# One of the four first-key one-hots of a group gathered by GpSimd from an identity matrix in DRAM

## The chip, the cores and the metric

The kernel runs on one core of a Trainium2 chip, in one launch. The metric is the device time of that launch in microseconds. All data are float32.

## The reference, cut to what matters

One encoder block over x of 1024 tokens by 1024: a Mamba-2 head group and an HGRN2 head group share an input and an output projection, then comes a PEER layer that picks experts by product keys, then a last RMSNorm. The change lies in the PEER layer:

```python
def peer_ffn(x, w_query, sub_keys, u_table, v_table):
    q = (xt @ w_query).reshape(t, PEER_HEADS, 2, PEER_HALF)
    s = jnp.einsum('thpd,hpnd->thpn', q, sub_keys)
    s_top, i_top = lax.top_k(s, PEER_TOPK)
    ...
    expert = idx1 * PEER_KEYS + idx2
    gate = jax.nn.softmax(c_top, axis=-1)
    def block(args):
        xb, eb, gb = args
        u = u_table[eb]
        hid = gelu(jnp.einsum('td,thkd->thk', xb, u)) * gb
        return jnp.einsum('thk,thkd->td', hid, v_table[eb])
```

There are 8 heads, 128 keys on each side (16384 experts) and 16 experts per token and head, so each token picks 128 experts, each with a first key, a second key and a gate.

## The kernel before, in words

The program runs stage after stage, each in its own block of instruction streams: input_norm, ssd, hgrn, mix_out, peer. The order of work within a stage is written out by hand, and engines wait on semaphores. The span of 3635 us divides into about 1127 us up to the end of hgrn, mix_out to about 1559 us, and peer.

**mix_out** multiplies by w_out (loaded by SP, L1313, after two small loads, L1309 and L1310), adds x, and routes the first 512 tokens on VectorE. GpSimd scatters the gates of token block 0 into the DRAM tensor sel (L1574), 16 indirect DMAs of 128 elements per head, and waits for each head's before the next.

**peer** treats the two halves of the tokens in different ways. The first 512 (blocks 0 to 3) go densely: for each first key e of 128, TensorE multiplies the tile u_cols[e] with the tokens (L1919), ScalarE takes gelu, VectorE multiplies by a tile of gates read from sel (L2125), and TensorE multiplies by v_cols (L1932) and VectorE adds (L2132). The other 512 go sparsely: GpSimd gathers, for a pick of each of 128 tokens, the 4 KB rows of u_rows (u_row, L1828) and v_rows (v_row, L1835) into two rings of 5 buffers; VectorE makes a dot product (L2138) and adds gate times row (L2149). Both run side by side, slot by slot, 256 slots.

Before the slots stands the **hot stage**, which the change touches. It fills sel for token blocks 1 to 3 (MB = 3), as a dense matrix of gates over first and second key for each token. A group j of 96 (M_GROUPS) takes 4 tokens. The partition is a pick of the token, the free index a key.

- VectorE (hot, from L2104) makes hot_a: one compare of 512 columns, 4 tokens by 128 keys, 1 where the key is the pick's first key (L2109). Then it makes three of the four hot_b: 1 where the key is the second key, times the gate (L2113).
- ScalarE (hot_last, L1972 and L1975) makes the fourth hot_b out of Abs and Relu.
- TensorE (L1900) multiplies the transposed hot_a with hot_b for each of the four tokens: a 128x128 matrix of gates in ps_o.
- ScalarE (place_out, L1988 and L1991) copies each half of it into a staging buffer. In its stream stand, for each group: place_out(j, 0), hot_last(j + 2), place_out(j, 1).
- SP stores a staging buffer of 2 MB to sel after each 16 groups (L1805), twice. hot_a, hot_b and ps_o have two buffers: VectorE's group j waits until TensorE has done group j - 2, and TensorE's group j until ScalarE has copied out group j - 2.

A block of 32 groups is one block of 128 tokens. Its picks are turned by TensorE (turn_picks, L1887) and copied by ScalarE (pick_copy, L1964 and L1965) into pickedT; the first two at the start, the third at group 40. After groups 24 and 60 VectorE routes a unit of the sparse half (about 10 us each), and TensorE and ScalarE stand still.

GpSimd does nothing in the hot stage but five u_row (from 1608 us, once the routing after group 24 has given their indices). Then it waits for the last store of sel, sel_out[3], and issues v rows. SP loads the first three tiles of u_cols into ut[0], ut[1], ut[2] during the last block (L1799); ut[2] is the tensor ut2. After the last stores it loads va (L1810). ScalarE loads the first tiles of sel (L2018) once all stores have landed.

Of the kernel before, what the change touches and what calls it, by code (L numbers as in the profile page):

```python
# [8 lines left out]
F32 = mybir.dt.float32  # L9
# [49 lines left out]
RING = 5  # L59
OB = 3  # L60
# [328 lines left out]
def ssd(nc, w, w_in, w_ssd, par, w_hg, lb_logits, C, hnT, Y, spent, hw, H):  # L389
# [4 lines left out]
    with ExitStack() as ctx:  # L394
# [3 lines left out]
        primed = []  # L398

        def plain_sem(name):  # L400
            return ctx.enter_context(nc.semaphore("ssd_" + name))
# [265 lines left out]
        def _(dve):  # L667
# [130 lines left out]
            groups(dve, body)  # L798


def hgrn(nc, w_hg, C, hnT, Y, osq, ysq, sel, sel_zeroed, H):
# [6 lines left out]
    with ExitStack() as ctx:  # L808
# [299 lines left out]
class Route:  # L1108
# [3 lines left out]
    def __init__(self, nc, ctx):  # L1112
# [32 lines left out]
        self.scattered, self.negated = sem("scattered"), sem("negated")  # L1145
# [93 lines left out]
def mix_out(nc, x, w_out, mix_w, ffn_w, w_route, sel, sel_zeroed, C, Y, osq, ysq, xnT, R):  # L1239
# [4 lines left out]
    with ExitStack() as ctx:  # L1244
# [61 lines left out]
        def _(sp):  # L1306
# [344 lines left out]
def peer(nc, w_route, u_cols, v_cols, u_rows, v_rows, fin_w, sel, C, Y, osq, hnT, R, out):  # L1651
# [4 lines left out]
    with ExitStack() as ctx:  # L1656
# [35 lines left out]
        hot_a = [mflat[:, i * 512:(i + 1) * 512].rearrange("p (q c) -> p q c", q=4) for i in range(2)]  # L1692
        hot_b = [mflat[:, 1024 + i * 512:1024 + (i + 1) * 512].rearrange("p (q c) -> p q c", q=4) for i in range(2)]
# [4 lines left out]

        stage = [wide(va[:]), wide(vb), Y[:, 0:4, D:MIX], vr[:, 0:4, :]]
# [23 lines left out]
        sel_out = [sem(f"sel_out{i}") for i in range(4)]  # L1723
        x_turned, x_out = sem("x_turned"), sem("x_out")
# [99 lines left out]
        def _(pool):  # L1824
# [14 lines left out]
            for r in range(RING):  # L1839
                u_row(r)  # L1840
# [12 lines left out]
        def _(pe):  # L1853
# [38 lines left out]
            for j in range(M_GROUPS):  # L1892
# [203 lines left out]
        def _(dve):  # L2096
# [7 lines left out]
            def hot(j):  # L2104
# [4 lines left out]
                nc.vector.tensor_tensor(hot_a[j % 2], R.count[:].unsqueeze(1).to_broadcast([P, 4, KEYS]),  # L2109
                                        pickedT[:, b % 2, 0, t:t + 4].unsqueeze(2).to_broadcast([P, 4, KEYS]),  # L2110
# [101 lines left out]
def block_program(nc, x, ln_w, w_ssd, par, w_hg, lb_logits, w_out, mix_w, ffn_w, w_route, u_cols, v_cols, u_rows, v_rows,  # L2212
                  fin_w, sel, out):
    with ExitStack() as ctx:
# [6 lines left out]
        with nc.sbuf_tensor("reset", [P, SEQ], F32) as reset, nc.sbuf_tensor("lmask", [P, LEVELS + 1, P], F32) as lmask:  # L2221
            C["reset"], C["lmask"] = reset, lmask
            with nc.sbuf_tensor("w_group", [P, KT, SSD_COLS], F32) as w_group, ExitStack() as held:
# [4 lines left out]
                ssd(nc, w_group, group_in, w_ssd, par, w_hg, lb_logits, C, hnT, Y, spent, hw, H)  # L2228
                hgrn(nc, w_hg, C, hnT, Y, osq, ysq, sel, sel_zeroed, H)
        R = Route(nc, ctx)  # L2230
        mix_out(nc, x, w_out, mix_w, ffn_w, w_route, sel, sel_zeroed, C, Y, osq, ysq, hnT, R)
        peer(nc, w_route, u_cols, v_cols, u_rows, v_rows, fin_w, sel, C, Y, osq, hnT, R, out)
# [59 lines left out]
```

## Time and profile before

| | |
|---|---|
| runs | 3635.82 us median of 3 (3635.19 to 3636.2) |
| profiled execution | 3637.07 us, its span 3635.3 us |
| TensorE (PE) busy | 3447.0 us, 95% |
| VectorE (DVE) | 2821.6 us, 78% |
| ScalarE (ACT) | 1075.0 us, 30% |
| GpSimd (POOL) | 1428.6 us, 39% |
| DMA | 829.65 MB, 228 GB/s on average |

PE is TensorE's matmuls, PEld its weight loads, SPq SyncE's DMA issues. L12 is line 12 of the kernel. Times in the rows are microseconds from the start of the span. The figure in brackets behind a row of the timeline is how long the engine had been idle before it, and what ended that. "issue" is time in which an engine waited for nothing that the profile shows. A duration on the timeline runs until the result is written, so the next instruction can start before it ends.

### The profile page before, as it was taken

The numbers are of one execution on the slowest core, as the hardware profiler recorded it, in microseconds if no ns is written. First come the engines' busy times: TensorE is split into PE (matmuls) and PEld (weight loads), VectorE is DVE, ScalarE is ACT, GpSimd is POOL, SyncE is SP. The second block draws the span as 40 slices with busy tenths as digits, with TensorE's granted clock in tenths as the row PEclk, the third lists the DMA queues.
The fourth block names the chain that finished last, engine by engine and source line by source line (L and its number), as shares of the span: only waits on it lengthen the run. The fifth ranks groups of instructions, "written<-read, shape, count | busy, mean of one in ns | idle before, by whom it ended". The sixth has DMA issues, their size and how long they took to land.

```text
span 3635.3 us, 39991 instructions
## 1 busy us (share of the span) xinstructions
PE 3447.0 (95%) x11593; PEld 1977.6 (54%) x11593; DVE 2821.6 (78%) x6530; ACT 1075.0 (30%) x2717; POOL 1428.6 (39%) x1233
## 2 busy tenths in 40 slices
PE   7999989999996999677899999999999999999998
PEld 4666667777774566456444444444444444444443
DVE  2466676777773489889698888987888889888897
ACT  3233344435452222278121112111211122121212
POOL 1000000000001277400466566655666666665664
PEclk9999999999997999889999999999999999999999
DMA  3111012001003233245999999999999999999998
GB/s 111 30 36 35 0 61 79 23 23 35 25 10 136 50 75 75 34 132 173 388 387 377 392 386 386 377 391 351 389 375 388 389 390 378 376 394 378 387 377 329
DMA packets 313936, 829.65 MB, mean 228 GB/s; under 512 B 41504, under 2 KB 145056, under 8 KB 305056
## 3 DMA queue, kind: packets, MB, share of 16 engines
q0 software_dynamic: 165888, 537.01, 39.9%
q1 hardware_dynamic: 125104, 227.45, 17.2%
q10 hardware_dynamic: 22768, 63.18, 4.5%
q8 instruction: 69, 1.13, 0.1%
q14 instruction: 107, 0.88, 0.1%
HBM read 789.73 MB, written 37.81 MB: 228 GB/s over the span
## 4 chain that ended last, share of the span: by engine, by line
PE 44%; issue 6%; DVE 4%; DMA 2%; POOL 1%; another core or an unknown queue 0%; ACT 0%; DVEq 0%; ACTq 0%; POOLq 0%
PE peer_ps_o L1932 21%; PE peer_ps_d L1919 20%; PE peer_ps_q L1860 2%; DMA peer_vr<-in_v_rows,peer_index 2%; DVE Y L2149 1%; DVE peer_ur L2138 1%; DVE peer_mt L2109 0%; POOL peer_ur L1828 0%; DVE peer_mt L2113 0%; POOL peer_vr L1835 0%; DMA peer_ur<-in_u_rows,peer_index 0%; PE peer_ps_s L1870 0%; DVE Y L2166 0%; DVE route_hit L1209 0%
## 5 line engine op out<-in xcount | busy, mean ns | idle before, releaser
L1828 POOL DMA_INDIRECT peer_ur<-in_u_rows,peer_index x512 | 569.4, 1112 | 606.3 <-DVE peer_ur L2138 396.8
L2149 DVE SCALAR_TENSOR_TENSOR Y<-peer_vr,peer_hid,Y 128x1024 f32<-128x1024 f32 x512 | 657.1, 1283 | 103.1 <-DMA peer_vr<-in_v_rows,peer_index 97.9
L1835 POOL DMA_INDIRECT peer_vr<-in_v_rows,peer_index x512 | 588.8, 1150 | 331.8 <-issue 149.0
L2138 DVE SCALAR_TENSOR_TENSOR peer_ur<-peer_ur,Y 128x1024 f32<-128x1024 f32 x512 | 628.0, 1227 | 9.7 <-DMA peer_ur<-in_u_rows,peer_index 7.9
L1919 PE MATMUL peer_ps_d<-hnT,route_ut 128*128 128x512 f32 x1376 | 598.5, 592 | 0.0
L1932 PE MATMUL peer_ps_o<-peer_va,Y 128*128 128x512 f32 x1024 | 445.0, 594 | 12.8 <-DVE Y L2125 12.8
L1932 PE MATMUL peer_ps_o<-hnT,Y 128*128 128x512 f32 x1024 | 442.6, 592 | 0.0
L1919 PEld LDWEIGHTS peer_ps_d<-hnT,route_ut 128*128 128x128 f32 x1376 | 261.3, 190 | 327.7 <-issue 327.7
L1932 PEld LDWEIGHTS peer_ps_o<-peer_va,Y 128*128 128x128 f32 x1024 | 194.9, 191 | 253.8 <-issue 236.1
L1932 PEld LDWEIGHTS peer_ps_o<-hnT,Y 128*128 128x128 f32 x1024 | 193.5, 190 | 238.2 <-issue 238.2
L1919 PE MATMUL peer_ps_d<-hnT,peer_ut 128*128 128x512 f32 x672 | 295.3, 592 | 0.0
L2006 ACT ACTIVATE peer_act_out<-peer_dots 128x2 f32<-128x2 f32 x256 | 51.2, 200 | 796.2 <-DVE peer_ur L2138 775.4
L1999 ACT ACTIVATE Y<-peer_ps_d 128x512 f32<-128x512 f32 x128 | 76.4, 597 | 672.2 <-PE peer_ps_d L1919 652.2
L1574 POOL DMA_INDIRECT sel<-route_ut,mo_sel_index x128 | 210.1, 1641 | 159.0 <-DVE route_ut L1217 89.1
L1375 PE MATMUL mo_ps_h<-mo_w,mo_yT 128*128 128x512 f32 x512 | 225.9, 599 | 8.2 <-DMA mo_w<-in_w_out 7.1
L512 PE MATMUL ssd_ps_piece<-hnT,w_group 128*128 128x512 f32 x512 | 226.8, 596 | 6.9 <-ACT hw L595 5.1
L1559 POOL IOTA mo_count_u<- 128x128 uint32 x1 | 0.2, 240 | 592.2 <-POOLq L808 592.2
L1919 PEld LDWEIGHTS peer_ps_d<-hnT,peer_ut 128*128 128x128 f32 x672 | 127.4, 190 | 159.3 <-issue 159.3
L494 POOL TENSOR_TENSOR ssd_awide<-ssd_a,tri 128x512 f32<-128x512 f32 x32 | 34.5, 1079 | 450.2 <-PE ssd_ps_rows L556 403.1
L894 PE MATMUL hg_ps_piece<-hnT,hw 128*128 128x512 f32 x448 | 199.7, 599 | 4.3 <-ACTq L1017 4.3
L898 PE MATMUL hg_ps_piece<-hw,hnT 128*128 128x256 f32 x896 | 198.0, 379 | 0.0
L898 PEld LDWEIGHTS hg_ps_piece<-hw,hnT 128*128 128x128 f32 x896 | 168.1, 190 | 21.7
(329 smaller groups left out, 4894.6 us busy)
## 6 DMA issues: line engine op xcount, KB each, us to landing
route_ut<-in_u_cols SPq DMA_DIRECT2D x86, 512.0 KB
peer_va<-in_v_cols SPq DMA_DIRECT2D x16, 2048.0 KB
peer_mt<-sel ACTq DMA_DIRECT2D x64, 512.0 KB
hnT<-in_v_cols SPq DMA_DIRECT2D x16, 2048.0 KB
peer_ut<-in_u_cols SPq DMA_DIRECT2D x42, 512.0 KB
route_wk<-in_w_route ACTq DMA_DIRECT2D x14, 1024.0 KB
hnT<-in_w_route SPq DMA_DIRECT2D x9, 1024.0 KB
route_wk<-in_w_route SPq DMA_DIRECT2D x9, 1024.0 KB
```

Of the source, the lines that this page charges most:

```text
L512: mm = nc.tensor.matmul(bank, w[:, k, i * P:(i + 1) * P], hnT[:, half, k, :], start=(k == 0), stop=(k == KT - 1))
L894: mm = nc.tensor.matmul(bank, w[:, kt, p * P:(p + 1) * P], hnT[:, half, kt, :], start=(kt == 0), stop=(kt == KT - 1))
L898: mm = nc.tensor.matmul(bank[:, 0:2 * P], hnT[:, half, kt, cols(p - 2)], w[:, kt, 2 * P:4 * P], start=(kt == 0), stop=(kt == KT - 1))
L1375: mm = nc.tensor.matmul(ps_h[:, half, :], yT[:, k, :], w[:, k, half * 512:(half + 1) * 512], start=(k == 0), stop=(k == MT - 1))
L1574: pool.indirect_dma_start(sel.rearrange("a i q two (t o) -> (a i q two t) o", o=1), bass.IndirectOffsetOnAxis(ap=sel_index[:, h, k:k + 1], ...
L1828: pool.indirect_dma_start(ur[:, r % RING, :], None, u_rows, bass.IndirectOffsetOnAxis(ap=index[:, r // TOPK % 4, r % TOPK:r % TOPK + 1], a ...
L1835: pool.indirect_dma_start(vr[:, r % RING, :], None, v_rows, bass.IndirectOffsetOnAxis(ap=index[:, r // TOPK % 4, r % TOPK:r % TOPK + 1], a ...
L1919: mm = nc.tensor.matmul(ps_d[:, e % 2, :], ut[e % UT][:, k, :], xT[:, k, :], start=(k == 0), stop=(k == KT - 1))
L1932: mm = nc.tensor.matmul(ps_o[:, o % OB, :], ht(e, tb), v_tile(e, half), start=(j == 0), stop=(j == GE - 1))
L1999: nc.scalar.activation(ht(e), ps_d[:, e % 2, :], ACT.Gelu).then_inc(gelu_done, 1)
L2138: nc.vector.scalar_tensor_tensor(out=ur[:, s, :], in0=ur[:, s, :], scalar=1.0, in1=Y[:, b, D:MIX], op0=ALU.mult, op1=ALU.mult, accum_out=d ...
L2149: nc.vector.scalar_tensor_tensor(out=hb, in0=vr[:, s, :], scalar=hid[:, c:c + 1], in1=hb, op0=ALU.mult, op1=ALU.add).then_inc(comb_done, 1)
```

## The change

The 128x128 identity, which lies in SBUF, is stored to a DRAM tensor eye at the beginning of mix_out, ahead of the loads of w_out. In the hot stage VectorE compares 384 columns for three tokens of a group; the fourth first-key one-hot is a gather by GpSimd: partition p gets row first_key[p] of eye, 512 bytes. The gathered one-hots go into a ring of 8 buffers, which lie in ut2. So the third tile of u_cols is loaded only after the last group's product. At the first group of each block VectorE copies the first keys as integers into first_place, and GpSimd waits for that copy. The five u_row move behind hot rows 86, 88, 90, 92 and 94 of GpSimd's stream. TensorE waits for the gathered row, too. The new semaphores need room: hgrn's SP clears those of ssd.

```diff
@@ peer, sync
                     sp.wait_ge(pick_turned, MB)
-                    for e in range(UT):
+                    for e in range(UT - 1):
                         sp.dma_start(ut[e], u_cols[e]).then_inc(u_in[e], 16)
...
             for i in range(2):
                 sp.wait_ge(sel_out[i], sel_stores(i))
+            sp.wait_ge(sel_made, M_GROUPS)
+            sp.dma_start(ut[UT - 1], u_cols[UT - 1]).then_inc(u_in[UT - 1], 16)
             sp.dma_start(va[:], v_cols[0, 0]).then_inc(v_in[0], 16)
@@ peer, gpsimd
-            for r in range(RING):
-                u_row(r)
+            def hot_row(j):
+                b, t = j // (P // 4), j % (P // 4) * 4 + 3
+                if t == 3:
+                    pool.wait_ge(place_ready, b + 1)
+                need(pool, sel_made, j - HOTS + 1)
+                pool.indirect_dma_start(hots[:, j % HOTS, :], None, eye,
+                                        bass.IndirectOffsetOnAxis(ap=first_place[:, b % 2, t:t + 1], axis=0)
+                                        ).then_inc(got_hot[j % HOTS], 16)
+
+            pool.wait_ge(R.eye_out, 16)
+            for j in range(M_GROUPS):
+                hot_row(j)
+                if j >= M_GROUPS - 2 * RING and j % 2 == 0:
+                    u_row((j - M_GROUPS) // 2 + RING)
             pool.wait_ge(sel_out[3], sel_stores(3))
@@ peer, tensor
                 need(pe, staged, 2 * (j - 1))
+                pe.wait_ge(got_hot[j % HOTS], 16 * (j // HOTS + 1))
                 for q in range(4):
-                    mm = nc.tensor.matmul(ps_o[:, j % 2, q * P:(q + 1) * P], hot_a[j % 2][:, q, :], hot_b[j % 2][:, q, :],
+                    first = hot_a[j % 2][:, q, :] if q < 3 else hots[:, j % HOTS, :]
+                    mm = nc.tensor.matmul(ps_o[:, j % 2, q * P:(q + 1) * P], first, hot_b[j % 2][:, q, :],
                                           start=True, stop=True)
@@ peer, vector
-                nc.vector.tensor_tensor(hot_a[j % 2], R.count[:].unsqueeze(1).to_broadcast([P, 4, KEYS]),
-                                        pickedT[:, b % 2, 0, t:t + 4].unsqueeze(2).to_broadcast([P, 4, KEYS]),
+                if t == 0:
+                    nc.vector.tensor_copy(first_place[:, b % 2, :], pickedT[:, b % 2, 0, :]).then_inc(place_ready, 1)
+                nc.vector.tensor_tensor(hot_a[j % 2][:, 0:3], R.count[:].unsqueeze(1).to_broadcast([P, 3, KEYS]),
+                                        pickedT[:, b % 2, 0, t:t + 3].unsqueeze(2).to_broadcast([P, 3, KEYS]),
                                         ALU.is_equal).then_inc(hot_a_ready, 1)
@@ mix_out, sync
             sp.dma_start(fw, ffn_w).then_inc(s_in, 16)
+            sp.dma_start(eye, C["ident"][:]).then_inc(R.eye_out, 16)
@@ hgrn, sync
             prime(sp, primed)
+            for s in used:
+                sp.sem_clear(s)
```

HOTS is 8, RING is 5, UT is 3.

## Rows read from the trace of the kernel before

**Rows 1.** The page's busy part, and TensorE's waits from 1721 to 1900 us (total, times, longest).

```profile
PE 3447.0 (95%) x11593; PEld 1977.6 (54%) x11593; DVE 2821.6 (78%) x6530; ACT 1075.0 (30%) x2717; POOL 1428.6 (39%) x1233
...
PE peer_ps_o L1932 <- DVE Y L2125: 9.7, 2, 7.9
```

**Rows 2.** Windows: from:to, length, each engine's busy us (instructions), granted clock, DMA share, GB/s.

```profile
1620.00:1661.00 41.00, 32.88 (x236) 28.18 (x235) 40.57 (x118) 40.00 (x119) 0.00 (x0) 1.00 0.71 205
```

**Rows 3.** Timeline of one group: start us, duration us, engine, line, operation, output<-input, count.

```profile
1640.99 0.38 ACT L1991 ACTIVATE peer_va<-peer_ps_o 128x256 f32<-128x256 f32 x1
1641.07 0.68 DVE L2109 TENSOR_TENSOR peer_mt<-route_count,peer_pickedT 128x512 f32<-128x512 f32 x1
...
1641.25 1.13 PE L1900 MATMUL peer_ps_o<-peer_mt 128*128 128x128 f32 x8 [0.30 <-DVE peer_mt L2113]
1641.27 0.39 ACT L1972 ACTIVATE peer_mt<-route_count,peer_pickedT 128x128 f32<-128x128 f32 x1
1641.67 0.85 DVE L2113 TENSOR_SCALAR peer_mt<-route_count,peer_pickedT 128x128 f32<-128x128 f32 x3
1641.70 0.49 ACT L1975 ACTIVATE peer_mt<-peer_mt,peer_pickedT 128x128 f32<-128x128 f32 x1
1642.10 0.36 ACT L1991 ACTIVATE hnT<-peer_ps_o 128x256 f32<-128x256 f32 x1
1642.42 0.38 ACT L1991 ACTIVATE peer_va<-peer_ps_o 128x256 f32<-128x256 f32 x1
```

**Rows 4.** Groups by form, 1530 to 1730 us: count, busy us, mean ns, idle before, releasers.

```profile
L2109 DVE TENSOR_TENSOR peer_mt<-route_count,peer_pickedT 128x512 f32<-128x512 f32 x96 | 66.1, 689 | 6.1 <-PE peer_ps_o L1900 4.5 <-ACT peer_pickedT L1965 1.3
```

**Rows 5.** Timeline of VectorE, ScalarE and TensorE at the stage's beginning.

```profile
1559.91 0.36 DVE L2172 CAST route_ut<-peer_first_key 128x384 f32<-128x384 uint32 x1
...
1560.31 0.56 DVE L2173 SCALAR_TENSOR_TENSOR route_ut<-route_ut 128x384 f32<-128x384 f32 x1
...
1561.89 0.27 ACT L1965 ACTIVATE peer_pickedT<-peer_ps_t 128x128 f32<-128x128 f32 x1
...
1564.71 5.26 PE L1900 MATMUL peer_ps_o<-peer_mt 128*128 128x128 f32 x24 [1.65 <-ACT peer_mt L1975]
```

**Rows 6.** Timeline: VectorE ends a dot product, GpSimd, already waiting, starts a gather.

```profile
1749.72 0.08 DVE L2138 DVE_READ_ACCUMULATOR peer_ur<-peer_ur,Y 128x1 f32 x1
...
1750.57 1.24 POOL L1828 DMA_INDIRECT peer_ur<-in_u_rows,peer_index  x1 [2.81 <-DVE peer_ur L2138]
```

**Rows 7.** GpSimd's timeline while it scatters: two issues that waited for earlier ones to land.

```profile
1271.06 1.89 POOL L1574 DMA_INDIRECT sel<-route_ut,mo_sel_index  x1 [2.27 <-DMA sel<-route_ut,mo_sel_index]
...
1339.94 1.54 POOL L1574 DMA_INDIRECT sel<-route_ut,mo_sel_index  x1 [4.98 <-DMA sel<-route_ut,mo_sel_index]
```

**Rows 8.** GpSimd's timeline, 1608 to 1615 us; VectorE's products there (min/median/max ns); page's software queue.

```profile
1608.39 1.54 POOL L1828 DMA_INDIRECT peer_ur<-in_u_rows,peer_index  x1 [89.74 <-DVE peer_index L2101]
...
1612.80 0.94 POOL L1828 DMA_INDIRECT peer_ur<-in_u_rows,peer_index  x1 [0.30 <-issue]
...
1614.04 1.37 POOL L1828 DMA_INDIRECT peer_ur<-in_u_rows,peer_index  x1 [0.30 <-issue]
...
L2113 DVE TENSOR_SCALAR peer_mt<-route_count,peer_pickedT x12: 339/342/476, 1609.0 to 1615.0; 128x128 f32<-128x128 f32 x12
...
q0 software_dynamic: 165888, 537.01, 39.9%
```

**Rows 9.** GpSimd's timeline: the first v row.

```profile
1739.35 0.94 POOL L1835 DMA_INDIRECT peer_vr<-in_v_rows,peer_index  x1 [123.94 <-DMA sel<-peer_vr]
```

**Rows 10.** Windows at the end of the stage.

```profile
1705.00:1720.00 15.00, 12.10 (x88) 10.29 (x86) 15.00 (x45) 14.64 (x44) 0.00 (x0) 1.00 0.98 291
...
1720.00:1722.00 2.00, 1.20 (x9) 1.04 (x9) 2.00 (x3) 1.16 (x4) 0.00 (x0) 1.00 0.04 16
```

**Rows 11.** SP's timeline at mix_out's beginning, and TensorE's waits from 1100 to 1240 us.

```profile
1127.97 0.43 SPq L1310 DMA_DIRECT2D route_ut<-in_ffn_w  x1
...
PE mo_ps_h L1375 <- DMA mo_w<-in_w_out: 7.1, 1, 7.1
```

More of the change, by code:

```diff
@@ L59 @@
 RING = 5
+HOTS = 8
 OB = 3
@@ L396, in sb @@
             return ctx.enter_context(nc.sbuf_tensor("ssd_" + name, shape, dt))
-        primed = []
+        primed, used = [], []
         def plain_sem(name):
-            return ctx.enter_context(nc.semaphore("ssd_" + name))
+            used.append(ctx.enter_context(nc.semaphore("ssd_" + name)))
+            return used[-1]
         def sem(name):
@@ L798, in _, with hgrn @@
             groups(dve, body)
-def hgrn(nc, w_hg, C, hnT, Y, osq, ysq, sel, sel_zeroed, H):
+    return used
+def hgrn(nc, w_hg, C, hnT, Y, osq, ysq, sel, sel_zeroed, H, used):
     with ExitStack() as ctx:
@@ L1144, in __init__ @@
             sem("best_ready"), sem("gates_ready"), sem("routed"), sem("gated"))
-        self.scattered, self.negated = sem("scattered"), sem("negated")
+        self.scattered, self.negated, self.eye_out = sem("scattered"), sem("negated"), sem("eye_out")
 D_CHOSEN, D_GATE, D_FIRST, D_SECOND = range(4)
@@ L1236, in now, with mix_out @@
         self.hold()
-def mix_out(nc, x, w_out, mix_w, ffn_w, w_route, sel, sel_zeroed, C, Y, osq, ysq, xnT, R):
+def mix_out(nc, x, w_out, mix_w, ffn_w, w_route, eye, sel, sel_zeroed, C, Y, osq, ysq, xnT, R):
     with ExitStack() as ctx:
@@ L1648, in _, with peer @@
             gate_of(DU - 1)
-def peer(nc, w_route, u_cols, v_cols, u_rows, v_rows, fin_w, sel, C, Y, osq, hnT, R, out):
+def peer(nc, w_route, u_cols, v_cols, u_rows, v_rows, fin_w, eye, sel, C, Y, osq, hnT, R, out):
     with ExitStack() as ctx:
@@ L1692, in peer @@
         hot_a = [mflat[:, i * 512:(i + 1) * 512].rearrange("p (q c) -> p q c", q=4) for i in range(2)]
+        hots = ut2[:].rearrange("p k c -> p (k c)").rearrange("p (s c) -> p s c", c=P)
         hot_b = [mflat[:, 1024 + i * 512:1024 + (i + 1) * 512].rearrange("p (q c) -> p q c", q=4) for i in range(2)]
@@ L1697, in wide @@
             return t.rearrange("p k c -> p (k c)").rearrange("p (e d) -> p e d", d=D)
+        first_place = first_key[:, 0:2 * P].rearrange("p (b t) -> p b t", b=2)
         stage = [wide(va[:]), wide(vb), Y[:, 0:4, D:MIX], vr[:, 0:4, :]]
@@ L1723, in peer @@
         sel_out = [sem(f"sel_out{i}") for i in range(4)]
+        got_hot, place_ready = [sem(f"got_hot{i}") for i in range(HOTS)], sem("place_ready")
         x_turned, x_out = sem("x_turned"), sem("x_out")
@@ L2212, in block_program @@
 def block_program(nc, x, ln_w, w_ssd, par, w_hg, lb_logits, w_out, mix_w, ffn_w, w_route, u_cols, v_cols, u_rows, v_rows,
-                  fin_w, sel, out):
+                  fin_w, eye, sel, out):
     with ExitStack() as ctx:
@@ L2227, in block_program @@
                 spent = input_norm(nc, x, ln_w, w_ssd, C, hnT, w_group, group_in)
-                ssd(nc, w_group, group_in, w_ssd, par, w_hg, lb_logits, C, hnT, Y, spent, hw, H)
-                hgrn(nc, w_hg, C, hnT, Y, osq, ysq, sel, sel_zeroed, H)
+                used = ssd(nc, w_group, group_in, w_ssd, par, w_hg, lb_logits, C, hnT, Y, spent, hw, H)
+                hgrn(nc, w_hg, C, hnT, Y, osq, ysq, sel, sel_zeroed, H, used)
         R = Route(nc, ctx)
-        mix_out(nc, x, w_out, mix_w, ffn_w, w_route, sel, sel_zeroed, C, Y, osq, ysq, hnT, R)
-        peer(nc, w_route, u_cols, v_cols, u_rows, v_rows, fin_w, sel, C, Y, osq, hnT, R, out)
+        mix_out(nc, x, w_out, mix_w, ffn_w, w_route, eye, sel, sel_zeroed, C, Y, osq, ysq, hnT, R)
+        peer(nc, w_route, u_cols, v_cols, u_rows, v_rows, fin_w, eye, sel, C, Y, osq, hnT, R, out)
 def laid_out(inputs):
@@ L2287 @@
     out = nc.dram_tensor("out_0", [1, SEQ, D], F32, kind="ExternalOutput").ap()
+    eye = nc.dram_tensor("eye", [P, P], F32).ap()
     sel = nc.dram_tensor("sel", [KEYS, KEYS // 2, DB * P // SELB, 2, SELB], F32).ap()
-    block_program(nc, sel=sel, out=out, **args)
+    block_program(nc, eye=eye, sel=sel, out=out, **args)
     r = run_bass_kernel_spmd(nc, [{"in_" + n: a for n, a in arrays.items()}], core_ids=[0])
```

## The prediction

> **What bounds the kernel now.** I read the page's first two parts, then the times of the stage that the change touches, then one group of that stage instruction by instruction, then the waits behind it. Over the whole span TensorE is busy 95% and VectorE 78% [rows 1], but that average says little about the stretch after 1562 us, in which the 96 groups of one-hots are made. In 41 us of it VectorE is busy 40.57 us and ScalarE 40.00, GpSimd not at all, TensorE 32.88 [rows 2]. So VectorE looks like the bound, and ScalarE stands 0.6 us in 41 behind it: both lie at their limit.
>
> One group shows why [rows 3]. VectorE starts the 512-wide compare at 1641.07 and the first of the three products at 1641.67; the whole stretch of [rows 2] holds 118 VectorE instructions, four to a group, so a group comes every 41 / 29.5 = 1.39 us; I use 1.40. ScalarE's four operations start at 1641.27, 1641.70, 1642.10 and 1642.42, and the round closes 0.28 us later, as from 1640.99 to 1641.27: 0.43 + 0.40 + 0.32 + 0.28 = 1.43, of which some is waiting. Its busy share says how much: 1.0 us free in 41, or 0.03 per group, so ScalarE's own round is about 1.37 us. TensorE's round with ScalarE is no shorter: a product starts at 1641.25, the first copy-out at 1642.42 (1.17 later), the second 1.11 after that, done 0.36 later, then the product two groups on: 2.64 us and a hand-over of about 0.1 for two groups, again 1.37 each.
>
> **The change, part by part.**
>
> *VectorE's compare.* 384 columns in place of 512. The 512-wide form takes 0.689 us [rows 4], and its time goes with its width (a 384-wide two-input operation took 0.56 [rows 5]): 0.13 us less per group, 12.8 us over 96 groups if VectorE alone set the pace (96 is the count in [rows 4]). It doesn't: from 1.40 the group can fall to ScalarE's 1.37 and no further. That is 0.03 x 96, **-3.0 us**. Bounds: -3.5 with the four groups after the two routing pauses, where VectorE works alone, and 0 if ScalarE keeps 1.40.
>
> *The three copies into first_place*, one per block of 32 groups. A 128x384 cast took 0.36 us [rows 5], so about 0.2 for 128 columns. They fall in VectorE's new slack; what they cost is the head of the gather's chain, counted next. Queued behind a copy is the compare of its own group.
>
> *The first gather of each block.* GpSimd now issues 96 gathers of 128 rows of 512 bytes. Within a block it runs up to 8 groups ahead, but at groups 0, 32 and 64 it must wait for place_ready, which VectorE gives only after group j-2 has left TensorE. The chain from VectorE's start: copy 0.2; hand-over from VectorE's end to a waiting GpSimd 0.77 (1749.80 to 1750.57), the issue 1.24 [rows 6]; landing. No row shows a 64 KB gather landing. The nearest is the scatter of as many rows: GpSimd, waiting for its landing, sat idle 2.27 us, 0.77 of it hand-over, so 1.5 [rows 7]. Taken as 1.5; bounds 0.5 (a load that costs little beyond its bytes) and 4.2 (the longest such wait of the scatter, 4.98, less the hand-over). With 0.1 for TensorE: 3.8 us. TensorE would have taken that group 1.55 us after VectorE's start (0.60 + 0.85 + 0.1 [rows 3]). Each of groups 32 and 64 is late by 2.25 us: **+4.5**, bounds +2.4 and +10. Group 0: picked at 1562.16, product at 1564.71 [rows 5], gathered row at 1562.2 + 3.8 = 1566.0: **+1.3**, bounds +0.3 and +4. Behind a late product stand ScalarE's copy-out and VectorE's group after next, both double-buffered, so nothing is won back.
>
> *GpSimd's pace.* Five gathers of 4 KB rows were issued in this very stage, from 1608.39 to 1614.04 [rows 8]: 1.41 us apart on average, the last step 1.24. They go by the row, not by its length: 165888 packets for 1152 indirect transfers, 144 each, of 4 KB and of 4 bytes alike. I take 1.27, near the last step, since the first holds a wake-up; it is below TensorE's 1.37, and a lead grows by 0.10 us per group.
>
> *The five gathers of u rows.* Before, they ran in the pause at 1608 to 1615 [rows 8], where nobody waited. Now one goes after each of hot rows 86, 88, 90, 92 and 94. From hot row 86 to 95 GpSimd issues 14 times, 17.8 us, where TensorE wants nine groups, 12.3 us: 5.5 short. The lead since group 64 is 22 x 0.10 = 2.2. **+3.3**, bounds +2.2 (1.24 a piece) and +7.4 (1.41, no lead).
>
> *The u tile and the end of the stage.* The third u_cols load now waits for the last product and goes on SP behind the last stores and ahead of va, which comes later by it; TensorE takes that tile third. Its 512 KB at the software queue's 537 MB / (0.399 x 3635 us) = 370 GB/s [rows 8] is 1.4 us, moved behind the stores. The u rows (2.6 MB, 7.1 us at 370) and the last dozen hot rows (0.8 MB, 2.7 us at 291) come into a stretch in which the DMA engines are busy 0.98, with a gap of 2 us from 1720 [rows 10]. 7.1 + 2.7 - 1.4 - 2 - 3.3 (the stage is longer by that) leaves 3.1 us by which the last stores may land later, and GpSimd's first v row, which started at 1739.35, waits for just those, as do the first sel tiles [rows 9]. TensorE stalls later for 9.7 us on VectorE's multiply, two times [rows 1]; there is no spare time there, so what DMA is late may pass on. I take **+2.0** of 3.1, because part of the gathers' packets fit between stores; bounds 0 and +6.
>
> *Storing the identity* takes one SP issue ahead of w_out, 0.43 us, and TensorE waited 7.1 us for that load [rows 11]: **+0.4**, bounds 0 and +0.6. The sem_clears stand on SP while heads run; SP's next load there waits for TensorE anyway: 0, and some 3 us on SP if that cover were gone.
>
> **Sum**: -3.0 + 4.5 + 1.3 + 3.3 + 2.0 + 0.4 = **+8.5 us**. The profiled execution took 3637.07 us for a span of 3635.3 and lies 1.25 above the median 3635.82; set on the median this is 3644.3.
>
> *A rule against this change.* In the hot stage, with GpSimd gathering, VectorE's products showed 339 / 342 / 476 ns (min, median, max) where they otherwise stay near 340, and GpSimd's issues 0.94 to 1.54 us [rows 8]: they touch each other, now and then. The Trainium skill (SBUF — State Buffer, "Who interferes with whom") says that a tensor_scalar in a two-port mode holds a port pair that GpSimd needs to write descriptors, and that the second to come is blocked to the end of the instruction. By that rule the three products of each group would shut GpSimd out for part of 0.77 us in every 1.37. The trace agrees only in part: the last spacing is still the bare 1.24.
>
> **The rivals.**
>
> *GpSimd sets the pace (0.16).* If each gather costs the mean of the five in this stage, 1.37 + 0.30 after the last included, (1615.71 - 1608.39) / 5 = 1.46 us, it decides from 1.40 upward: 84 groups without a stored lead lose 0.06 each, 5.0; the u rows cost 14 x 1.46 - 9 x 1.40 = 7.8; nothing is gained at VectorE. 5.0 + 7.8 + 4.5 + 1.3 + 2.0 + 0.4 = +21.0, 3656.8. For it: the sample is from this stage. Against: its first step holds a wake-up. This is the mechanism of the skill's rule above.
>
> *Everything lands in the shadow (0.20).* All lower bounds: -3.5 + 2.4 + 0.3 + 2.2 = +1.4, 3637.2. For it: the load is small. Against: the scatter's 2.27.
>
> *VectorE was the whole bound (0.12), not slower than before.* If ScalarE's round shortens once VectorE is out of the way (it decides below about 1.30 us per group), the full 12.8 us are earned; the smallest latencies, 2.7, go off, and the u rows cost 17.4 - 9 x 1.27 - 0.7 = 5.3: -4.8, 3631.0; with the u rows hidden too it is -10.1. For it: VectorE's 40.57 of 41. Against: ScalarE's starts leave 0.03 us free per group. That the narrower compare isn't shorter is excluded by [rows 5].
>
> **How the numbers follow.** The forecast's own case has 0.52 and spreads over +4 to +15. A measurement of this kernel tells 0.2%, 7.3 us, from no change. Slower by more: 0.40 of the forecast's case and 0.16 of the GpSimd case, 0.56. Within: 0.12 of the forecast's, 0.20, and 0.05 of the last, 0.37. Faster by more: the rest of the last, 0.07. The range 3634 to 3657 takes in the shadow case, the forecast's whole spread and half of the GpSimd case; what is left out is most of the last rival and the other half, about 0.2.
>
> **What would show it.** In the changed profile: the compare near 0.55 us; ScalarE, not VectorE, without idle time in the stage, groups 1.37 us apart; three waits of TensorE's hot product for a DMA into the hots, some 1 to 2 us, at groups 0, 32 and 64, and more of them in the last ten groups; GpSimd's steps near 1.27; sel's last store landing 8 us later or more; the stall on VectorE's product around 1808 no shorter. I am wrong if those waits are absent, if the group falls well below 1.37, or if GpSimd's steps exceed 1.40.

## The result, and the profile after

The changed kernel took **3668.34 us** (median of 6, 3663.95 to 3671.78) against 3636.01 (median of 6, 3634.16 to 3640.13) in the same set: +32.3 us, a ratio of 1.0081 [1.007, 1.0091]. The forecast was 3644.3, +8.5, with a range from 3634 to 3657: slower, as said, but nearly four times as much. The profiled execution took 3668.46 us for a span of 3666.6; before it was 3637.07 and 3635.3.

The page's busy part, then the groups by form from 1560 to 1760 us (count, busy us, mean ns, idle time before and its releasers), of the changed kernel:

```profile
PE 3461.5 (94%) x11593; PEld 1989.4 (54%) x11593; DVE 2819.2 (77%) x6533; ACT 1076.4 (29%) x2717; POOL 1528.2 (42%) x1329
...
L1855 POOL DMA_INDIRECT peer_ut<-eye,peer_first_key x96 | 101.4, 1056 | 113.8 <-DVE peer_first_key L2135 85.0 <-issue 17.4 <-PE peer_ps_o L1925 11.4
...
L2140 DVE TENSOR_SCALAR peer_mt<-route_count,peer_pickedT 128x128 f32<-128x128 f32 x288 | 87.7, 362 | 0.0
L2136 DVE TENSOR_TENSOR peer_mt<-route_count,peer_pickedT 128x384 f32<-128x384 f32 x96 | 53.6, 558 | 30.0 <-PE peer_ps_o L1925 28.0
```

The compare fell from 689 to 558 ns, as forecast [rows 4], 12.5 us less in all. But VectorE's idle time ahead of it rose from 6.1 to 30.0 us, 28.0 of it waiting for TensorE. TensorE's waits in the same stretch (total, times, longest) name the new one:

```profile
PE peer_ps_o L1925 <- DMA peer_ut<-eye,peer_first_key: 15.2, 12, 2.8
```

To see where the time went, I took the start of each group's compare from both timelines. How much later it starts than in the kernel before is its lag, and the lag grows in steps. It is 3.05 us at group 0, 4.19 at group 3, 6.87 at 30, **12.90 at 36**, 14.22 at 63, **19.35 at 69**, 19.98 at 84, **24.48 at 93**, 26.3 at SP's last issue of sel, and 31.3 at the end of the span. Groups 32 and 64 are the first of a block. A group's compare waits for the product two groups before, so a product that is late at 32 shows at compare 34. The timeline around group 32:

```profile
1626.66 0.23 DVE L2135 CAST peer_first_key<-peer_pickedT 128x128 uint32<-128x128 f32 x1
...
1627.16 1.01 POOL L1855 DMA_INDIRECT peer_ut<-eye,peer_first_key  x1 [18.32 <-DVE peer_first_key L2135]
...
1628.48 1.12 POOL L1855 DMA_INDIRECT peer_ut<-eye,peer_first_key  x1 [0.30 <-PE peer_ps_o L1925]
1628.56 4.04 SPq L1814 DMA_DIRECT2D sel<-Y  x4
...
1629.81 1.62 PE L1925 MATMUL peer_ps_o<-peer_mt 128*128 128x128 f32 x6 [1.69 <-DMA peer_ut<-eye,peer_first_key]
...
1632.64 2.60 SPq L1814 DMA_DIRECT2D sel<-peer_vr  x1
...
1634.27 1.62 PE L1925 MATMUL peer_ps_o<-peer_mt 128*128 128x128 f32 x6 [2.42 <-DMA peer_ut<-eye,peer_first_key]
```

The first gather of the block lands before 1629.81, 1.6 us after its issue ended. The **second** one, issued at 1628.48, runs beside four stores of 512 KB and one of 2 MB that SP issues from 1628.56 on: TensorE gets it at 1634.27, 4.7 us after its issue ended. The lag grows by 2.3 us from compare 33 to 34, which is the first gather, and by 3.1 from 34 to 35, which is the second. And TensorE then works slowly. Windows of that stretch (from:to, length, busy us of PE, PEld, DVE, ACT, POOL with counts, granted clock, DMA share, GB/s):

```profile
1626.00:1633.00 7.00, 3.73 (x21) 3.11 (x20) 4.69 (x16) 4.51 (x13) 4.62 (x5) 0.75 0.53 147
1633.00:1640.00 7.00, 5.68 (x26) 5.45 (x27) 3.23 (x10) 3.28 (x10) 5.16 (x7) 0.52 1.09 315
```

A clock of 0.52 is close to the lower level, 1.2 of 2.4 GHz. In windows of 2 us it is 1.00 from 1624 to 1628 and 0.50 from 1630 to 1638, so it fell around the first wait, of 1.69 us: six matmuls take 1.62 us there, 0.91 otherwise. Not every wait of this length is followed by the lower level: the last one below is 1.79 us long, and its six matmuls take 0.91. At the end of the stage rows are late again, beside the loads of the first two u tiles, the stores of sel and the u rows:

```profile
1725.14 13.28 SPq L1808 DMA_DIRECT2D route_ut<-in_u_cols  x2
...
1737.78 0.95 POOL L1839 DMA_INDIRECT peer_ur<-in_u_rows,peer_index  x1 [0.30 <-issue]
1739.04 1.26 POOL L1855 DMA_INDIRECT peer_ut<-eye,peer_first_key  x1 [0.30 <-PE peer_ps_o L1925]
1746.38 0.91 PE L1925 MATMUL peer_ps_o<-peer_mt 128*128 128x128 f32 x6 [1.79 <-DMA peer_ut<-eye,peer_first_key]
```

The last gathered row needs 6.1 us from the end of its issue to TensorE.

### The profile page after: what moved, and what is told of

It is laid out like the page before. It is cut to its first block, busy times and chain, and to the rows that moved or that the text cites. A ratio compares the mean times of both kernels' runs of the same rounds, so it can differ in the third digit from the quotient of the medians.

```text
span 3666.6 us, 40125 instructions
## 1 busy us (share of the span) xinstructions
PE 3461.5 (94%) x11593; PEld 1989.4 (54%) x11593; DVE 2819.2 (77%) x6533; ACT 1076.4 (29%) x2717; POOL 1528.2 (42%) x1329
## 4 chain that ended last, share of the span: by engine, by line
PE 50%; DVE 2%; issue 2%; DMA 2%; ACT 1%; POOL 0%; DVEq 0%; ACTq 0%; POOLq 0%
PE peer_ps_o L1957 24%; PE peer_ps_d L1944 22%; PE peer_ps_q L1883 2%; PE peer_ps_o L1925 2%; DMA peer_vr<-in_v_rows,peer_index 1%; DMA peer_ut<-eye,peer_first_key 0%; DVE peer_mt L2140 0%; DVE Y L2176 0%; DMA peer_ur<-in_u_rows,peer_index 0%; PE peer_ps_s L1893 0%; ACT peer_mt L2000 0%; DVE peer_mt L2136 0%; ACT peer_mt L1997 0%; DVE peer_ur L2165 0%; POOL peer_vr L1846 0%
## 5 line engine op out<-in xcount | busy, mean ns | idle before, releaser
L1957 PE MATMUL peer_ps_o<-peer_va,Y 128*128 128x512 f32 x1024 | 449.0, 598 | 13.8 <-DVE Y L2152 13.8
```

The lines of the kernel that those rows point to most:

```text
L1957: mm = nc.tensor.matmul(ps_o[:, o % OB, :], ht(e, tb), v_tile(e, half), start=(j == 0), stop=(j == GE - 1))
```

## The experiments

Each is told against the kernel before in its own set (medians 3638.6, 3638.2 and 3638.3 us). Three repairs, called mends here, each of one wait, were run alone and in all combinations. **U**: the five u rows issued early. **P**: the first keys of all blocks cast early. **R**: the ring of gathered rows in a tile of its own.

**The most that could be saved** (the fourth place's one-hot of the first key is left out):

```diff
-                nc.vector.tensor_tensor(hot_a[j % 2], R.count[:].unsqueeze(1).to_broadcast([P, 4, KEYS]),
+                nc.vector.tensor_tensor(hot_a[j % 2][:, 0:3], R.count[:].unsqueeze(1).to_broadcast([P, 3, KEYS]),
...
-                    mm = nc.tensor.matmul(..., hot_a[j % 2][:, q, :], hot_b[j % 2][:, q, :],
+                    mm = nc.tensor.matmul(..., hot_a[j % 2][:, q % 3, :], hot_b[j % 2][:, q, :],
```

> The kernel before with the comparison alone cut from 512 to 384 numbers a group; the fourth product uses the first one-hot again, so the fourth place's one-hot of the first key is left out of the computation; no gather, no identity matrix, nothing on GpSimd. It shows the most that the change can save. Theory of the prediction: VectorE is freed of 0.13 us a group, but the group is then bound by ScalarE at 1.37 instead of 1.40, so it saves 3.0 us: 3633.0. Rival 'VectorE was the whole bound': 96 x 0.133 = 12.8 us saved, 3623. Rival 'nothing is saved, the pair VectorE - TensorE - VectorE sets the pace': 3635 to 3637.

Measured: 3638.44 us, ratio 0.9998 [0.9989, 1.0007]. **Nothing.** Windows from 1638 to 1658 us, the kernel before and then this one, columns as above:

```profile
1638.00:1658.00 20.00, 15.96 (x114) 13.55 (x112) 19.99 (x59) 19.52 (x59) 0.00 (x0) 1.00 0.65 186
```

```profile
1638.00:1658.00 20.00, 16.19 (x116) 13.74 (x114) 19.07 (x59) 19.52 (x59) 0.00 (x0) 1.00 0.65 184
```

VectorE has 0.93 us of slack and ScalarE is as full as it was, with as many instructions. TensorE's waits from 1620 to 1661 us show who ends last, in the kernel before and then in this one:

```profile
PE peer_ps_o L1900 <- DVE peer_mt L2113: 7.4, 27, 0.3
```

```profile
PE peer_ps_o L1900 <- ACT peer_vr L1991: 3.7, 14, 0.3
PE peer_ps_o L1900 <- ACT hnT L1991: 3.6, 14, 0.3
```

TensorE waits just as long as before, 7.3 us in 28 waits, but for ScalarE and no longer for VectorE. ScalarE's round with TensorE is the bound; which of the two sets its length no run separates. The lag of the compares went from +0.93 at group 0 to -0.22 at group 93, so 1.15 us were won in the stage, not 3.0 and not 12.8.

**U alone, and all three** (U, P and R in this order):

```diff
-                if j >= M_GROUPS - 2 * RING and j % 2 == 0:
-                    u_row((j - M_GROUPS) // 2 + RING)
+                if j == P // 4 - 1:
+                    for r in range(RING):
+                        u_row(r)
...
-                if t == 0:
-                    nc.vector.tensor_copy(first_place[:, b % 2, :], pickedT[:, b % 2, 0, :]).then_inc(place_ready, 1)
+                if j in PLACE_AT:
+                    n = PLACE_AT.index(j)
+                    dve.wait_ge(pick_out, n + 1)
+                    nc.vector.tensor_copy(first_place[:, n, :], pickedT[:, n % 2, 0, :]).then_inc(place_ready, 1)
...
-        hots = ut2[:].rearrange("p k c -> p (k c)").rearrange("p (s c) -> p s c", c=P)
+        hots = vr[:, 4, :].rearrange("p (s c) -> p s c", c=P)
...
-            sp.wait_ge(sel_made, M_GROUPS)
-            sp.dma_start(ut[UT - 1], u_cols[UT - 1]).then_inc(u_in[UT - 1], 16)
```

> The changed kernel with one move: the five dense u rows are issued by GpSimd in one go behind the gather of group 31, while it waits for the second block's picks, and no longer two groups apart among the last ten gathers. Theory 'late operands' (the +32.3 us of the change are rows that land late, each at its own place): the end of the stage, where VectorE's lag on the kernel before grew from 19.35 at group 69 to 24.48 at group 93 and 26.3 at the last store, loses the u rows' part, and the time falls by 6 to 8 us against the changed kernel, to 3660 to 3662. Rival 'GpSimd sets the pace' (95 issues of 1.06 us each at any place): the five issues are moved into a wait of GpSimd, which gives 5 x 1.1 = 5.5 us at the end and takes them at the boundary of group 32, so the sum stays within 2 us of 3668. Rival 'one pool of transfers' (the DMA engines and not GpSimd are late at the end): within 2 us of 3668 too, but with the waits of TensorE's last six groups as long as they are now (6.6 us).

> The changed kernel with the three mends together: u rows early, the three blocks' first keys copied at groups 0, 2 and 44, the ring of gathered one-hots in the fifth v tile and the last u tile loaded with the others as before the change. Theory 'late operands' takes off the borders (10.8 us), the u rows (6) and the u tile in the dense part (2 to 5): 3668.3 - 20 = 3648, range 3643 to 3652, still slower than before (3636.0) by the pace, the first gather and the start. Rival 'contention': the pace of 1.45 us and the waits return elsewhere, 3658 to 3668. Rival 'the offload pays once its waits are gone': below 3636.

Measured: U alone 3659.23 (+20.7, ratio 1.0056 [1.0042, 1.007]); all three 3648.91 (+10.3, 1.0031 [1.0019, 1.0043]), as the theory had it. U's theory said 6 to 8 us off the changed kernel; against the kernel before in each set it is 11.7, so the place was right and the size too small. Both rivals of U, within 2 us of 3668, fell. Two thirds of the loss go when the same operations stand in other places; a third stays, and no version beats the kernel before.

**P alone and R alone.**

> The changed kernel with one move: the three blocks' first keys are cast at groups 0, 2 and 44, into three slots, instead of at the first group of each block, so that GpSimd can issue the gathers of a block while TensorE is still in the one before. With the u rows early and all three mends the time was 3648.9 (before: 3638.6 in the same set), with the u rows early alone 3659.2. Theory 'late at the borders': the steps of 5.7 us at groups 33 to 36 and 5.1 us at 65 to 69 in VectorE's lag shrink to under 1.5 us each, and the time falls by 8 to 10 us against the changed kernel, to 3658 to 3660. Rival 'a transfer behind a store is late at any place': the steps move to other groups, and the time falls by under 4 us.

> The changed kernel with the ring of gathered one-hots in the fifth v tile, so that the third u tile's load stands with the first two again and SP doesn't wait for the 96th group. Theory 'the u tile is late in the dense part': 2 to 5 us off the changed kernel, 3663 to 3666. Rival 'its load is hidden behind the va load anyway': within 1.5 us of the changed kernel; the +5.0 us that the dense part showed in the profiled execution would then be the v rows or a difference between executions.

Measured: P 3664.22 (+26.0), R 3681.86 (+43.6, **worse** than no mend by 11 us). P took off 6.3 us where its theory said 8 to 10, and R's theory missed the sign, so the other pairs were run.

> The changed kernel with two of the three mends: u rows early and the blocks' first keys early; the ring of one-hots stays in the last u tile, which is loaded behind the 96th group. Measured so far against the kernel before: no mend +32.3, u rows early +20.7, first keys early +26.0, ring apart +43.6, all three +10.3. Theory 'the mends of u rows and borders add up, and the ring apart gives back what the late u tile costs (2.9 us in the dense part)': +32.3 - 11.7 - 6.3 = +14, within 2 us of +13 (all three, plus 2.9), so 3651 to 3654. Rival 'TensorE's late completions (1.1 to 3.5 us, seen with the first keys early alone and with the ring apart alone) come and go with the arrangement': a value outside +9 to +18, with such gaps in the trace.

> The changed kernel with u rows early and the ring apart; the first keys of each block are cast at its first group. Theory 'transfers in the same place': with the u rows early the third u tile's load has only the stores and gathers beside it, and the time is that of u rows early alone less the late u tile's 2.9 us, plus what the load costs the last gathers: +18 to +24, 3656 to 3662. Rival 'the earlier load of the third u tile makes the gathers late by itself' (as ring apart alone, +11.3 on the changed kernel): +28 to +34, 3666 to 3672. With all three mends the same load is there at +10.3, which speaks against it.

> The changed kernel with first keys early and the ring apart, the u rows two groups apart at the end. Theory 'the mends add up with all three at +10.3': this is all three without the u rows' mend, which was worth 9 to 12 us: +19 to +22, 3657 to 3660. Rival 'the late completions of TensorE belong to GpSimd issuing u rows among the gathers' (both kernels that showed them did that; all three and u rows early did not): above +24, 3662 or more, with gaps of over 1 us between TensorE's last matmul of a group and the release of VectorE.

Measured: UP 3652.37 (+14.0), UR 3658.09 (+19.8), PR 3652.75 (+14.4). UP and UR came out as their theories had it, the rivals of all three fell, and PR did better than its theory. The lags of the compares on the kernel before, in us, from the timelines of one execution each:

```
            group 0     9    30    36    63    69    84    93   time
no mend        3.05  5.16  6.87 12.90 14.22 19.35 19.98 24.48  +32.3
U              3.49  5.69  7.50 13.47 14.81 19.84 20.51 22.00  +20.7
P              1.71 10.55 11.73 12.69 14.88 15.87 17.45 25.35  +26.0
R              0.75  9.52 10.70 17.96 22.96 32.34 37.52 41.48  +43.6
UP            -0.01  1.04  6.18  6.61  7.68  8.87  9.21  9.72  +14.0
UR            -1.28 -0.01  3.78  9.70 10.91 16.59 17.45 17.76  +19.8
PR             1.12  2.02  7.03  7.31  8.27  8.55  8.96 10.16  +14.4
UPR           -0.27  1.59  4.42  4.94  6.73  7.91  8.27  8.75  +10.3
```

The borders are settled: from group 30 to 36 the four kernels without P lose 5.9 to 7.3 us, the four with it 0.3 to 1.0; from 63 to 69 it is 5.0 to 9.4 against 0.3 to 1.2. The u rows show between 84 and 93: 1.2 to 7.9 us without U, 0.3 to 1.5 with it. What R is worth hangs on the other two: +11.3 alone, -11.6 on P, -0.9 on U, -3.7 on UP. A step in the middle of a block is new: UP and PR lose 4.0 and 4.2 us from compare 20 to 21, UR and UPR 2.9 and 1.5 from 21 to 22, where no mend and U lose 0.2 or less. So with P the late rows left the borders and in part came back elsewhere; what that step is, the next pair of kernels shows. P alone and R alone have something that the other six lack, here ahead of the compare of group 5 in P alone (start, duration, and the idle time with its releaser):

```profile
1577.32 0.62 PE L1926 MATMUL peer_ps_o<-peer_mt,peer_ut 128*128 128x128 f32 x2
...
1579.84 0.39 ACT L2017 ACTIVATE peer_va<-peer_ps_o 128x256 f32<-128x256 f32 x1 [3.51 <-remote]
1579.91 0.56 DVE L2139 TENSOR_TENSOR peer_mt<-route_count,peer_pickedT 128x384 f32<-128x384 f32 x1 [3.55 <-remote]
1580.07 1.21 POOL L1856 DMA_INDIRECT peer_ut<-eye,peer_first_key  x1 [1.26 <-remote]
```

TensorE's last matmul of the group ends at 1577.94, all eight being on record, and three engines that wait for it go on together only 1.9 us later. Such gaps are 1.1 to 3.5 us long, three in P's trace and three in R's; by group 9, where both have lost 8.8 us, they are 3.1 and 3.5 us of it. Part of the rest goes with TensorE's clock: after this gap it is granted 0.50 from 1578 to 1586 us. They don't come with issuing u rows among the gathers, since PR does that too and has none. What they are stays open, and with it why R alone costs 11 us.

**Gathers without use, and plain loads without use.** Both have the three mends, compare 512 numbers and let TensorE wait for a slot of the ring that it then doesn't read:

```diff
-                    first = hot_a[j % 2][:, q, :] if q < 3 else hots[:, j % HOTS, :]
+                    first = hot_a[j % 2][:, q, :]
...
-                pool.indirect_dma_start(hots[:, j % HOTS, :], None, eye,
-                                        bass.IndirectOffsetOnAxis(ap=first_place[:, b, t:t + 1], axis=0)
-                                        ).then_inc(got_hot[j % HOTS], 16)
+                pool.dma_start(hots[:, j % HOTS, :], eye).then_inc(got_hot[j % HOTS], 16)
```

(the second hunk in the second kernel only)

> The changed kernel with three mends (u rows early; the first keys of all three blocks copied at groups 0, 2 and 44, so that GpSimd can run ahead over a block's border; the ring of gathered one-hots in a v tile instead of the last u tile), and with VectorE comparing all 512 numbers again: TensorE still waits for each gather but multiplies with VectorE's own one-hot. So the gathers are pure addition. Theory 'late operands': with the borders mended hardly a gather is late, and what is left is the +2.9 us that are there before the stage, +1.2 for the first gather, +2 of pace: 3640 to 3645, and 3 us above the kernel with the same three mends that compares 384. Theory 'contention' (gathers, stores and VectorE slow each other at any place): the pace stays 1.45 us a group, and the time is 3655 to 3665.

> As e5_gather_unused (512 compared, three mends, 3651.7 against 3638.6), but GpSimd issues a plain load of the identity matrix into the same slot of the ring, with the same waits, in place of each indirect gather: the same bytes, no row addresses to be worked out. In e5 the three products of VectorE that fall beside a gather last 0.95 us together instead of 0.85 (mean of one 365 ns instead of 342), while the comparison keeps its 690 ns. Theory 'GpSimd at work on addresses slows VectorE's products': the mean goes back to 342 to 345 ns, and the drift between groups 36 and 60 falls from 1.5 us to under 0.5; the time to 3642 to 3647. Rival 'it is the rows being written': the mean stays at 360 or more and the time at 3650 to 3653.

Measured: gathers 3651.69 (+13.1, 1.0035 [1.0021, 1.0048]), plain loads 3645.85 (+7.6, 1.0021 [1.0011, 1.003]). The first lies between its two theories (3640 to 3645 and 3655 to 3665), the second in its theory's range. By the medians gathering costs 5.5 us more than loading the same bytes, though the two intervals overlap. First the timeline with gathers, then with loads:

```profile
1641.23 1.14 POOL L1854 DMA_INDIRECT peer_vr<-eye,peer_first_key  x1 [0.30 <-issue]
1641.47 0.95 DVE L2142 TENSOR_SCALAR peer_mt<-route_count,peer_pickedT 128x128 f32<-128x128 f32 x3
```

```profile
1641.13 0.85 DVE L2140 TENSOR_SCALAR peer_mt<-route_count,peer_pickedT 128x128 f32<-128x128 f32 x3
...
1641.95 0.54 POOL L1854 DMA_DIRECT2D peer_vr<-eye  x1 [0.82 <-PE peer_ps_o L1923]
```

From 1628 to 1655 us all 15 triples of products that lie 0.89 us or more beside an indirect issue took 0.95, the 4 that lie beside it for less 0.85 to 0.87, and with plain loads all 18 took 0.85 or 0.86. By itself that doesn't separate the kinds of issue, since a plain one lasts only 0.54 us and hardly reaches into the products. But the same trace with plain loads has products wholly beside each kind, four triples beside u rows and two beside runs of plain issues; one of each:

```profile
1610.89 1.55 POOL L1838 DMA_INDIRECT peer_ur<-in_u_rows,peer_index  x1 [8.07 <-DVE peer_index L2124]
1611.46 1.01 DVE L2140 TENSOR_SCALAR peer_mt<-route_count,peer_pickedT 128x128 f32<-128x128 f32 x3
...
1617.93 2.23 POOL L1854 DMA_DIRECT2D peer_vr<-eye  x4
1618.87 0.85 DVE L2140 TENSOR_SCALAR peer_mt<-route_count,peer_pickedT 128x128 f32<-128x128 f32 x3
```

The four beside indirect issues took 0.94 to 1.01, the two beside plain ones 0.85. So it is the indirect issue on GpSimd that goes with the slowing, and not the rows being written. But its price came out wrong: the drift between groups 36 and 60 fell only from 1.51 to 1.24 us, not below 0.5. Most of the 5.5 us is one transfer, that of group 19, with gathers:

```profile
1591.86 1.15 POOL L1854 DMA_INDIRECT peer_vr<-eye,peer_first_key  x1 [0.30 <-issue]
...
1592.92 5.09 SPq L1815 DMA_DIRECT2D sel<-hnT  x1
...
1593.32 1.13 POOL L1854 DMA_INDIRECT peer_vr<-eye,peer_first_key  x1 [0.30 <-issue]
...
1599.31 0.98 PE L1925 MATMUL peer_ps_o<-peer_mt 128*128 128x128 f32 x3 [3.58 <-DMA peer_vr<-eye,peer_first_key]
```

The row came 6.3 us after its issue ended, beside the store of 2 MB that SP issued at 1592.92, and the lag rose from 3.35 to 7.60 between groups 20 and 21. It could come late because GpSimd had no lead: from group 5 to 19 each of its gathers followed the last at once, 1.45 us apart, as far as the groups themselves, and only two gathers ahead of the compare. The plain loads, issued six ahead, show no such wait.

**No gather at all; the store moved.**

```diff
-            for j in range(M_GROUPS):
-                hot_row(j)
-                if j >= M_GROUPS - 2 * RING and j % 2 == 0:
-                    u_row((j - M_GROUPS) // 2 + RING)
+            for r in range(RING):
+                u_row(r)
...
-            sp.dma_start(eye, C["ident"][:]).then_inc(R.eye_out, 16)
...
             load_x(0)
+            sp.dma_start(eye, C["ident"][:]).then_inc(R.eye_out, 16)
```

(the first hunk in the first kernel, with 512 compared and no wait for a row; the others in the second)

> The changed kernel without any gather: VectorE compares 512 numbers as before, TensorE takes its own one-hots and waits for no row, GpSimd issues the five u rows as before; what stays of the change is the identity matrix's store, the semaphores and their clearing, the three casts, and the third u tile's load behind the 96th group. Theory 'what stands outside the gathers is real' (start of the stage +3.05, dense part +5.0 in the profiled execution): the time is 3641 to 3646 where the kernel before has 3636 to 3639. Rival 'both are differences between executions, a gather late or not': within 1.5 us of the kernel before, and all of the +32 us belongs to the gathers.

> The kernel with all three mends, with the identity matrix stored behind the loads of the output weights, the first keys and x, and no longer ahead of them. In every kernel that stores it ahead of them TensorE's wait for the output weights was 8.2 to 9.4 us, in the two that don't 7.0 and 7.1. Theory 'the store delays the weights': the wait is back at 7.1 and 1.8 us are saved, +8.5 instead of +10.3: 3646 to 3648. Rival 'it is covered by later waits': the same +10.3, within 0.7 us.

Measured: no gather 3644.61 (+6.4, 1.0017 [1.0008, 1.0027]), as its theory had it; the identity stored later (with all three mends) 3649.37 (+11.0, 1.003 [1.0019, 1.004]), no gain on +10.3. TensorE's wait for the output weights, in the changed kernel and with the store moved:

```profile
PE mo_ps_h L1381 <- DMA mo_w<-in_w_out: 9.2, 1, 9.2
```

```profile
PE mo_ps_h L1381 <- DMA mo_w<-in_w_out: 7.3, 1, 7.3
```

The wait was 7.1 before [rows 11] and lies between 7.6 and 9.6 in the eleven kernels that store the matrix first (the expectation's 8.2 to 9.4 overlooked the 7.6 and the 9.6). The store does lengthen the wait, and moving it mends the wait and not the time. Without gathers the lag was 1.92 at group 0 and 3.21 at group 93, 7.5 at the end of the span. Most of it thus comes after the hot stage, where the third u tile is late. One row of 1024 matmuls there is longer, before and without gathers:

```profile
L1932 PE MATMUL peer_ps_o<-peer_va,Y 128*128 128x512 f32 x1024 | 445.0, 594 | 12.8 <-DVE Y L2125 12.8
```

```profile
L1954 PE MATMUL peer_ps_o<-peer_va,Y 128*128 128x512 f32 x1024 | 447.9, 597 | 13.9 <-DVE Y L2149 13.9
```

This is 2.9 + 1.1 us; the changed kernel has 4.0 + 1.0:

```profile
L1957 PE MATMUL peer_ps_o<-peer_va,Y 128*128 128x512 f32 x1024 | 449.0, 598 | 13.8 <-DVE Y L2152 13.8
```

But the busy time of that row is no measure of the tile: the kernel that only compares 384 has 448.5 us in it, its u tile on time, and over the traces of all fourteen kernels it lies anywhere between 444.8 and 449.2. What was lost after the compare of group 95 tells more. It is 3.4 to 6.4 us, 4.6 in the mean, in the five changed kernels with the tile late, and -0.4 to 4.8, 2.2 in the mean, in the eight with it on time, from one execution each. So an estimate for the late tile is some 2 us, and no single pair of kernels shows it cleanly.

## Why the prediction was wrong, step by step

The direction came out, and the waits for rows stand where the forecast put them: at the first group of each block and among the last ten. Two terms of its sum failed most: the gain of 3.0 at VectorE, which is not there, and the +4.5 for the borders of the blocks, which were 11.1. The lags of the changed kernel add up to 31.3 us, the difference of the two spans, and stand against the forecast's terms so:

- **VectorE's compare and the pace, -3.0: measured +4.6** (3 to 30, 36 to 63 and 69 to 84: 2.7 + 1.3 + 0.6). This is the largest miss, 7.6 us. Two things failed. The gain itself isn't there: the group sat at ScalarE's and TensorE's round of about 1.39, not 1.37, and the compare alone saves 0.1 us of time. The 0.03 us per group were read as slack from a busy share of 97.6%, and that share didn't move when VectorE's work shrank. And with gathers the groups come about 0.05 us further apart; the products' stretching from 0.85 to 0.95 is real, but plain loads without it drift nearly as much, so what spaces the groups is open. The forecast had called that stretching something that happens now and then; in the kernel before, all four triples beside the five u rows took 0.94 to 0.99.
- **The first gather, +1.3: measured +1.1** (group 0 to 3). Right; its landing, 1.7 us here and 1.6 at group 32, was near the 1.5 taken.
- **The blocks' borders, +4.5: measured 11.1** (6.0 + 5.1). This is the second miss, 6.6 us. "Each of groups 32 and 64 is late by 2.25 us" priced the first gather only, on free DMA engines, and for that one it was right at group 32: 2.3 (1.5 at group 64). The second ran beside SP's stores and cost 3.1 more (2.3 at group 64), because without a lead nothing covers a landing of 4.7 us, and TensorE at its lower clock took 1.62 us for 0.91 us of work. Its upper bound, +10, was nearer than the value taken.
- **GpSimd's pace of 1.27: too short.** Steps of 1.25 occur, but the mean issue took 1.06 us, with 0.30 behind it 1.36, and from hot row 72 to 86 the steps were 1.44, beyond the 1.40 that the forecast had named as a sign of being wrong. The lead that was to grow by 0.10 us a group stayed at four gathers and then three. Still the rival that GpSimd sets the pace fails for this kernel: from group 36 to 63 the lag grows by 1.3 us only, with the ring nearly full. In the kernel with unused gathers its pace did take the lead away, as told.
- **The u rows, +3.3: measured 6.3** (4.5 from 84 to 93, 1.8 to the last store). The issues were counted, 17.8 us for fourteen, and took 18.7. Not counted were the 2.6 MB that they put beside the one-hots on the same engines: the last row took 6.1 us to land. U alone took 11.7 us off the time, but it moves issues and bytes together, so the two are not told apart.
- **The u tile and the end, +2.0: measured 5.0**, of which 4.0 stand in the busy time of one row of matmuls (445.0 to 449.0 us) and 1.0 in the longer stall. By the fourteen traces that row varies as much whatever the tile does, so a part of this is a difference between executions, as told.
- **The store, +0.4: the lag at group 0 is +3.05.** The store put 2.1 us on its wait here and 0.5 to 2.5 in the others, and nothing of that is shown in the time. The start of the stage lay between -1.3 and +3.5 us in the twelve kernels with the store, eleven of which are the same program up to there, and at +0.9 in the one that only compares 384 and has no store. So most of that term is a difference between executions.

The rivals: "VectorE was the whole bound" is excluded by the compare alone. "Everything lands in the shadow" falls with 15.2 us of waits for rows. "GpSimd sets the pace" named the right engine for the slowed products. The Trainium skill (SBUF — State Buffer, "Who interferes with whom") has whoever comes second blocked for the whole instruction of the other. The traces agree that the two engines touch, and show less than that: VectorE's triple grows by 0.10 us and GpSimd's issue from 0.94 to 1.14, both by less than one product of 0.34 lasts. Whether either is shut out for a moment they don't show. By that price the case would have cost 96 x 0.10 = 9.6 us at most, had VectorE been the bound.

## What to carry to other kernels

Before moving work off an engine that looks full, delete that work and time the rest: here the whole offload could save nothing, because a second engine was 97.6% busy in the same round. Issue a small transfer that an engine waits for several groups ahead, across every border of a loop; count its lead in the worst landing (here 6.3 us, beside stores), not the usual one (1.6 us), and check that the issuing engine is fast enough to build that lead. Moving other transfers next to it can cost more than their issues: here they were counted at 3.3 us, and 11.7 came back when they were moved away.

## What the runs showed of the hardware

- Three VectorE products took 0.95 us instead of 0.85 beside GpSimd's indirect issue and 0.85 beside plain ones, and the 512-wide compare of two tensors was untouched (690 ns with gathers, 689 before). A plain load's issue on GpSimd took 0.54 us, an indirect one 0.94 to 1.55.
- A gather of 64 KB was ready for TensorE 1.6 to 1.7 us after its issue where the DMA engines were 0.32 to 0.36 busy, and 4.7 to 6.3 us after it beside stores or loads of 2 MB and more.
- After a wait of 1.69 us TensorE's granted clock was 0.50 from 1630 to 1638 us, and six matmuls took 1.62 us; after another of 1.79 us they took 0.91.
- In two kernels of eight with nearly the same instructions TensorE's completions seem to reach the engines that wait for them 1.1 to 3.5 us late, three times in a stage. In the trace this is an idle time mostly put down to "remote". It was not explained.
